# Output projection and queries in one block, a norm by one value per token, gate products written interleaved, and a later wait for the gathered tokens

## The reference, cut to what matters

```python
merged = sigmoid(z_ga) * (o_a @ w_o_attn) + sigmoid(z_gb) * (o_b @ w_o_lru)
x = x + gate1 * (merged @ w_out)                       # output projection
h2 = rms_norm(x, norm2_w) * (1 + scale2) + shift2      # norm over the 1024 channels of a token
q = (h2 @ w_q)                                         # 8 heads x 2 halves x 128: 16 query units
s = q . keys                                           # 128 scores per token, head and half
top_s, top_i = top_k(s, 16)                            # then 16 of the 16 x 16 pairs: expert, gate
act = gelu(h2 . u[expert]);  y = sum(gate * act * v[expert])
x = x + gate2 * y
```

## Time and profile before

| | us |
|---|---|
| three runs, median (lowest, highest) | 3951.05 (3950.67, 3953.24) |
| the profiled execution, its own time | 3958.0 |
| its span, first to last instruction | 3956.2 |
| PE busy | 3665.3 (93%) |
| DVE, ACT, POOL busy | 2632.0 (67%), 1363.8 (34%), 592.2 (15%) |
| mean granted PE clock, of full speed | 0.962 |

### The profile page before, as it was taken

The page is one execution under the profiler, slowest core; times in us unless marked ns, Lnnn a source line. Parts: engine busy times, 40 slices in busy tenths (PEclk is TensorE's granted clock), DMA queues, the critical chain, the costliest instruction groups (busy, mean ns, idle before and its releaser), DMA issues. The chain is left out here.

```text
span 3956.2 us, 60630 instructions
## 1 busy us (share of the span) xinstructions
PE 3665.3 (93%) x21828; PEld 3400.2 (86%) x21828; DVE 2632.0 (67%) x5338; ACT 1363.8 (34%) x1755; POOL 592.2 (15%) x516
## 2 busy tenths in 40 slices
PE   5999998897797897999999999999889999999999
PEld 2777776786586797999999999999889999999999
DVE  5134443588334686687777777777577877788887
ACT  3134343476212211233333342424233333333332
POOL 0000000000000000222222323231122222222221
PEclk8999999899798898999999999999999999999999
DMA  7311110110422112667776868595799999999997
GB/s 282 127 62 63 47 51 35 41 67 32 149 107 91 54 51 93 221 202 244 236 258 221 270 210 280 198 298 183 247 374 347 346 347 347 350 369 348 346 346 270
DMA packets 372800, 811.92 MB, mean 205 GB/s; under 512 B 30720, under 2 KB 207744, under 8 KB 369152
## 3 DMA queue, kind: packets, MB, share of 16 engines
q1 hardware_dynamic: 298880, 540.81, 38.9%
q0 software_dynamic: 73728, 268.47, 19.9%
HBM read 679.66 MB, written 129.50 MB: 205 GB/s over the span
## 5 line engine op out<-in xcount | busy, mean ns | idle before, releaser
L80 PE MATMUL s_ps_a<-back_dense_hi,s_u_hi 128*128 128x384 f32 x2048 | 708.9, 346 | 43.7 <-DVE s_u_lo L1648 26.8
L80 PE MATMUL c_ps_y<-c_wa_hi,c_v_hi 128*128 128x384 f32 x2048 | 686.6, 335 | 29.3 <-DVE c_wa_lo L1984 29.3
L82 PE MATMUL s_ps_a<-back_dense_hi,s_u_lo 128*128 128x384 f32 x2048 | 691.1, 337 | 0.0
L81 PE MATMUL s_ps_a<-back_dense_lo,s_u_hi 128*128 128x384 f32 x2048 | 690.8, 337 | 0.0
L81 PE MATMUL c_ps_y<-c_wa_lo,c_v_hi 128*128 128x384 f32 x2048 | 685.2, 335 | 0.0
L82 PE MATMUL c_ps_y<-c_wa_hi,c_v_lo 128*128 128x384 f32 x2048 | 685.1, 335 | 0.0
L1962 ACT ACTIVATE c_v_hi<-c_v_raw 128x1024 fp32r<-128x1024 f32 x256 | 271.7, 1061 | 658.2 <-PE c_ps_y L82 624.6
L1585 POOL DMA_INDIRECT s_row<-in_u_rows,back_expert x128 | 159.7, 1248 | 2045.1 <-DVE back_expert L1750 1603.7
L1982 DVE TENSOR_TENSOR c_v_lo<-c_v_raw,c_v_hi 128x1024 fp32r<-128x1024 f32 x256 | 313.7, 1225 | 195.3 <-ACT c_v_hi L1962 195.1
L80 PEld LDWEIGHTS s_ps_a<-back_dense_hi,s_u_hi 128*128 128x128 f32 x2048 | 390.2, 191 | 45.4 <-DVE s_u_lo L1648 27.0
L80 PEld LDWEIGHTS c_ps_y<-c_wa_hi,c_v_hi 128*128 128x128 f32 x2048 | 385.2, 188 | 30.4 <-issue 25.9
(11 more groups left out here) (329 smaller groups left out, 6704.2 us busy)
## 6 DMA issues: line engine op xcount, KB each, us to landing
c_v_raw<-in_v SPq DMA_DIRECT2D x256, 512.0 KB, 6.3
s_u_raw<-in_u SPq DMA_DIRECT2D x128, 512.0 KB, 4.9
act_scratch<-s_a SPq DMA_DIRECT2D x128, 384.0 KB, 3.9
gm_scratch<-s_gm SPq DMA_DIRECT2D x48, 1024.0 KB
c_a<-act_scratch SPq DMA_DIRECT2D x256, 192.0 KB, 3.5
c_g<-gm_scratch SPq DMA_DIRECT2D x256, 192.0 KB, 4.3
a_w<-in_w_ada SPq DMA_DIRECT2D x24, 1024.0 KB, 7.7
q_raw<-in_w_pq SPq DMA_DIRECT2D x17, 512.0 KB, 3.3
```

The costliest lines, as they stand in the source:

```text
L80: nc.tensor.matmul(out, w_hi, x_hi, start=first, stop=False)
L81: nc.tensor.matmul(out, w_hi, x_lo, start=False, stop=False)
L82: return nc.tensor.matmul(out, w_lo, x_hi, start=False, stop=last)
```

## The change

1. project and route become one block, project_and_route. Its buffers share space: q takes x's, the keys those of the square and the sum, all_best, all_place, tok and struck take chunks of x1.
2. The norm: eight products of total's token tiles by a column of ones give one sum per token; root and reciprocal are taken of 128 x 8 values; DVE spreads them (copy by broadcast), PE transposes 8 tiles into ps_rstd, and DVE multiplies the chunks by PSUM.
3. DVE interleaves the multiplication of chunk k + 2 with the low parts of chunk k, and PE runs the first query unit chunk by chunk (512 and 256 dense columns) behind them, then its gathered columns.
4. Query weights 8 and 9 (units 0 and 1) are loaded and split in the projection. Unit u's scores are made between the two banks of unit u + 1. The token tiles are transposed after unit 0 and in unit 1, both through score[:, 1].
5. top16 writes all_best itself; the seventeenth weight is no longer loaded (nor the tenth of w_out laid out again).
6. A gate product writes every fourth column of ps_g, so that ACT copies runs of four tokens.
7. combine: tok is loaded after chunk 0 and waited for before the first gathered row; PE waits for the identity only at the last chunk.

```diff
-def project(nc, io, keep):
-def route(nc, io, keep):
+def project_and_route(nc, io, keep):
+        ps_ms, ps_rstd = score[:, 0, 0:TT], score[:, 1]
+        keys = sums[:].rearrange("p a (u n) -> p (a u) n", n=NK)
+        q = x
+        all_best, all_place = (x1[:, n:n + 2].rearrange(...) for n in (0, 2))
+        @block.sync
+            def load(n):
+                if n >= LOADED + 2:
+                    sp.wait_ge(lo_done, n - LOADED - 1)
+                sp.dma_start(raw[:, n % 2], weight(n)...).then_inc(raw_in[n % 2], 16)
+            for n in range(KD):
+                sp.wait_ge(x1_done, n + 1)
+                sp.dma_start(io["x1_scr"][n], x1[:, n]).then_inc(stored, 16)
+            load(KD + LOADED)
+            load(KD + LOADED + 1)
+            sp.wait_ge(spread_done, 1)
+            sp.dma_start(keys, ...).then_inc(keys_in, 16)
+            for n in range(KD + LOADED + 2, WEIGHTS):
+                load(n)
+        @block.scalar
+            nc.scalar.activation(root[:], ps_ms, ACT.Sqrt, bias=eps[:], scale=1.0 / D).then_inc(root_done, 1)
...
+            for u in range(UNITS):
+                for c, (c0, c1) in enumerate(split_columns(T)):
+                    act.wait_ge(half_done, 2 * u + c + 1)
+                    if u >= 2:
+                        act.wait_ge(s_ready, u - 1)
+                    nc.scalar.activation(q[:, u % 2, c0:c1], acc[:, u % 2, c0:c1], ACT.Copy).then_inc(q_done, 1)
+                    if u == 1 and c == 0:
+                        token_rows(1)
+                if u + 2 < UNITS:
+                    high(KD + u + 2)
+                if u == 0:
+                    token_rows(0)
+        @block.vector
+            low(KD - 1 + LOADED)
+            dve.wait_ge(root_done, 1)
+            nc.vector.reciprocal(rstd[:], root[:]).then_inc(rstd_done, 1)
+            nc.vector.tensor_copy(spread..., rstd[:]....broadcast_to([P, TT, P])).then_inc(rstd_done, 1)
+            dve.wait_ge(stored, 16 * KD)
+            dve.wait_ge(spread_done, 1)
+            normalise(0)
+            normalise(1)
+            for k in range(KD):
+                if k + 2 < KD:
+                    normalise(k + 2)
+                for n, (hi, lo, tokens) in enumerate(halves(k)):
+                    dve.wait_ge(h2_hi_done, 2 * k + n + 1)
+                    nc.vector.tensor_tensor(lo, tokens, hi.bitcast(F32), ALU.subtract).then_inc(h2_lo_done, 1)
+            for u in range(UNITS):
+                if u + 2 < UNITS:
+                    low(KD + u + 2)
+                hold(dve, s_ready, u + 1, passed)
+                top16(... all_best[:, t, u, 8 * g:8 * g + 8] ...)
+                nc.vector.tensor_copy(all_place[:, :, u], place[:]).then_inc(kept, 1)
+        @block.tensor
+            for j in range(TT):
+                last = nc.tensor.matmul(ps_ms[:, j:j + 1], total[:, j * P:(j + 1) * P], ones[:], start=True, stop=True)
+            for j in range(TT):
+                last = nc.tensor.transpose(ps_rstd[:, j * P:(j + 1) * P], spread[:, j * P:(j + 1) * P], ident[:])
+            for k in range(KD):
+                pe.wait_ge(h2_lo_done, 2 * k + 1)
+                for c0, c1 in ((0, HALF), (HALF, TD)):
+                    last = query(0, k, c0, c1)
+            pe.wait_ge(h2_lo_done, 2 * KD)
+            for k in range(KD):
+                last = query(0, k, TD, T)
+            token_rows(0)
+            for u in range(1, UNITS):
+                pe.wait_ge(lo_done, KD + u - LOADED + 1)
+                if u >= 2:
+                    pe.wait_ge(q_done, 2 * (u - 1))
+                bank(u, 0).then_inc(half_done, 1)
+                if u == 2:
+                    pe.wait_ge(tok_done, GATHERED)
+                scores(u - 1)
+                if u == 1:
+                    pe.wait_ge(tok_done, 1)
+                    token_rows(1)
+                bank(u, 1).then_inc(half_done, 1)
+            scores(UNITS - 1)
+    nc.clear_and_free_semaphores(sems)
+    nc.all_engine_barrier()
...
-                        nc.scalar.activation(gm[:, :, g * GT:(g + 1) * GT].rearrange("p i t -> p t i"),
-                                             ps_g[:, g % 2].rearrange("p (t i) -> p t i", t=GT), ACT.Copy).then_inc(g_copied, 1)
+                        nc.scalar.activation(gm[:, :, g * GT:(g + 1) * GT],
+                                             ps_g[:, g % 2].rearrange("p (i t) -> p i t", t=GT), ACT.Copy).then_inc(g_copied, 1)
...
-                                last = nc.tensor.matmul(ps_g[:, g % 2, i * NK:(i + 1) * NK], one2[:, g % 2, i], one1[:, g % 2, i], start=True, stop=True)
+                                last = nc.tensor.matmul(ps_g[:, g % 2].rearrange("p (n t) -> p n t", t=GT)[:, :, i], one2[:, g % 2, i], one1[:, g % 2, i], start=True, stop=True)
...
-            for s in range(RING):
+            load(0, 0, 0)
+            sp.dma_start(tok[:], io["tok_scr"][1]).then_inc(tok_in, 16)
+            for s in range(1, RING):
                 load(0, s, s)
-            sp.dma_start(tok[:], io["tok_scr"][1]).then_inc(tok_in, 16)
...
-                    dve.wait_ge(tok_in, 16)
...
                         if h == 0:
+                            dve.wait_ge(tok_in, 16)
...
+                if last:
+                    pe.wait_ge(consts_in, 16)
...
-            pe.wait_ge(consts_in, 16)
...
-                project(nc, io, keep)
-            route(nc, io, keep)
+                project_and_route(nc, io, keep)
```

More of the change, by code:

```diff
@@ L1381, in _ @@
             act.wait_ge(ident_in, 16)
             nc.scalar.activation(ident_r[:], ident[:], ACT.Copy).then_inc(ident_done, 1)
[L1383 to L1397 removed]
+            act.wait_ge(summed, 1)
@@ new lines, in _ @@
+            nc.scalar.activation(root[:], ps_ms, ACT.Sqrt, bias=eps[:], scale=1.0 / D).then_inc(root_done, 1)
+            for k in range(KD + 1):
+                if k < KD:
+                    act.wait_ge(normed, k + 1)
+                    nc.scalar.activation(x1[:, k], x1[:, k], ACT.Identity, bias=keep.mod[:, 3 * KD + k:3 * KD + k + 1],
+                                         scale=keep.gain[:, 2, k:k + 1]).then_inc(modulated, 1)
+                if k >= 1:
+                    act.wait_ge(modulated, k)
+                    for hi, _, tokens in halves(k - 1):
+                        nc.scalar.activation(hi, tokens, ACT.Copy).then_inc(h2_hi_done, 1)
@@ L1419, in _ @@
         @block.tensor
         def _(pe):
-            pe.wait_ge(ident_done, 1)
-            for g in range(GATHERED):
+            for n in range(KD):
+                if n >= LOADED:
+                    pe.wait_ge(lo_done, n - LOADED + 1)
+                    pe.wait_ge(x1_done, n - 1)
                 for k in range(KD):
-                    out, tile = score[:, g, k * P:(k + 1) * P], (TD + g * P, TD + (g + 1) * P)
+                    for c0, c1 in split_columns(T):
+                        last = product3(nc, acc[:, n % 2, c0:c1], w_hi[:, n % 2, k], w_lo[:, n % 2, k], keep.mg_hi[:, k, c0:c1], keep.mg_lo[:, k, c0:c1],
+                                        k == 0, k == KD - 1)
+                last.then_inc(prod_done, 1)
@@ new lines, in query, with bank, token_rows @@
+            def query(u, k, c0, c1):
+                return product3(nc, acc[:, u % 2, c0:c1], w_hi[:, u % 2, k], w_lo[:, u % 2, k], *h2(k, c0, c1), k == 0, k == KD - 1)
+            def bank(u, n):
+                for c0, c1 in TOKEN_BANKS[n]:
+                    for k in range(KD):
+                        last = query(u, k, c0, c1)
+                return last
+            def token_rows(g):
+                for k in range(KD):
+                    out, tile = score[:, 1, k * P:(k + 1) * P], (TD + g * P, TD + (g + 1) * P)
@@ L2125, in layout @@
     out["w_out"] = again(chunks(a["w_out"][0], P), 2)
-    out["w_pq"] = again(chunks(a["peer_w_q"][0], P))
+    out["w_pq"] = chunks(a["peer_w_q"][0], P)
     out["keys"] = np.ascontiguousarray(a["peer_keys"][0].transpose(3, 0, 1, 2)).reshape(P, -1)
```

281 lines of the change are left out of this document (107 added, 174 removed).

## The result

The changed kernel takes 3910.21 us (median of 4 runs, 3908.56 to 3911.43), against 3952.14 us before (4 runs, 3950.67 to 3958.04). The ratio is 0.9891, interval 0.9874 to 0.9908: 42 us faster, where 26 were forecast, and 1.8 us under the lower end of the range.

What follows compares the result with a forecast made beforehand. TensorE, busy 93% of the span, was taken as the bound. Routing -17.4 us, gate products 0 and combine -8 made -25.4: 3932.6 for the profiled execution, 7 us less for the median, forecast as 3925; range 3912 to 3948.

Steps and rivals of the forecast that it cites:

- The norm: Start of the routing: first sum product to first multiplication takes 6.9 us instead of 10.7, 3.8 less.
- Chunks and first unit: Routing's start: last dense subtraction 20.2 us behind first multiplication, high clock from 1296.3, unit 1 at 1298.1 (1295.5 to 1300.5).
- Units: Routing's other query units: still 13.07 us each, moved scores counted as nothing; last query product 20.4 us earlier.
- The new tail: End of the routing: the moved scores make the last top-16 start later, 2.7 us given back.
- The boundary: End of the joint block: clearing semaphores and a barrier cost 0 to 0.8 us, taken as 0.3.
- Gate products: Gate stage: ScalarE's copy may fall from 1110 to 600 ns, worth nothing since ScalarE waits for TensorE; taken as 0.
- The strided write: Gate stage: TensorE writing PSUM at a stride of four elements costs 0, or about 20 us at 0.120 per pass.
- (b): Gate stage: the strided write runs at half rate and pays 0.120 us per pass, +20 us, 3945; chance 0.13.
- (c): Gate stage: the strided write doubles the pass, 0.101 to 0.2 us, +130 us, 4055; chance 0.15.
- Combine: Combine's start: first product 11.2 us earlier, 2.4 to 3 us lost at chunk 4; taken -8, bounds -3 and -11.
- Rival (a): Combine gains nothing, as TensorE's early start is lost to transfers; -17.4 us in all, 3933; chance 0.10.
- The sum: Whole kernel: routing -17.4 us and combine -8 make -25.4 us.

Runs made afterwards that it cites:

- Experiment 9: The changed kernel with a plain first query unit, started only when all chunks are split: 3917.83 us, ratio 0.9916 to the kernel before.
- experiment 8: The changed kernel with unit 14's scores issued ahead of unit 15's first half: 3905.56 us, ratio 0.9886 to the kernel before.
- experiments 1: The kernel before with the gate edit alone (interleaved write and copy in runs of four): 3933.87 us, ratio 0.9959.
- 2: The kernel before with only ScalarE's gate copy made contiguous, TensorE's write as before, gates left in another order: 3930.87 us, ratio 0.9950.
- 3: The kernel before with only TensorE's gate write at a stride of four, ScalarE reading strided and writing as before: 3950.39 us, ratio 1.0000.
- 4: The kernel before with only ScalarE's order changed, next weight copy ahead of the fourth gate copy and activation: 3914.04 us, ratio 0.9906.
- experiment 7: The changed kernel with combine's 2 MB load of x1 issued behind each pass's chunk loads: 3903.22 us, ratio 0.9879 to the kernel before.
- experiment 6: The changed kernel with gate and combine edits undone, leaving the joint block alone: 3931.50 us, ratio 0.9951 to the kernel before.
- experiment 5: The kernel before with the combine edit alone (c_tok issued fourth, later waits for it and the identity): 3948.60 us, ratio 0.9993.

## Why the prediction was wrong in size, point by point

- **The norm: right.** -3.8 forecast, -4.3 measured between the last projection product and the first multiplication (14.46 to 10.17 us). Scaling the first stage's rows held but for the sums (2.94 us, 3.5 forecast): root and reciprocal 0.27 and 0.20, spreading copy 0.69, transposes 1.94 us.
- **Chunks and first unit: right mechanism, the clock mis-sized.** The last dense subtraction ended 20.3 us behind the first multiplication (20.2 forecast), with VectorE pacing at 2.33 us for a chunk. But unit 1 began 26.2 us behind it, not 28.7. I had counted the clock's rise from the unbroken work near 1289.6. But at the low clock the six products of a chunk nearly fill VectorE's 2.33 us: from the first query product, 1272.32, TensorE works with no recorded wait for three chunks, and the clock rises in the third, 5.6 us after that product. The trace has 512-column products 0.43 us apart until 1277.91 and 0.24 apart from 1279.57 on. Only then, with the products shorter, does TensorE wait, before each of the next four chunks (0.45, 1.02, 1.02 and 0.80 us), and the granted clock stays at 0.99 over 1278 to 1287. The 24 gathered products took 2.9 us, the value for the high clock. Experiment 9 gives the interleaving 9.4 us.
- **Units: right.** 196.9 us from the start of unit 1 to the last scores (197.9 forecast); no product waits.
- **The new tail: right.** The last top-16 starts 5.14 us behind the last scores, VectorE ends 15.46 us behind them (15.4 forecast), and experiment 8 takes 2.75 us of it back. The boundary costs 0.6 us more, where 0.3 was taken.
- **Gate products: the step that failed** is "is worth nothing: ScalarE waits 324.3 us for TensorE there". The 324.3 us are a sum over the stage. At the end of each chunk ScalarE works without a pause, and there what comes off the copy comes off the start of `s_u_hi`, of `s_u_lo`, of `s_one` and of TensorE's late group (0.51 us off the copy, 0.42 us off the group's start). The row for the wait was in hand, 24.0 us in 42 pieces with VectorE as releaser; it was used only as a deduction from the strided write's price, and I did not ask what VectorE was waiting for. The runs showed 17.7 us gained where the term was 0: experiments 1 and 2 show the gain (16 and 19 us), 3 that the write has no part in it, and 4 that the order in ScalarE's queue is the cause, since with the weight copy ahead of the fourth, still long, copy only 0.8 of the 35.7 us are left. The remaining 4.5 us by which this stage differs between the two profiled executions are the clock between the bodies, and no step of the prediction.
- **The strided write: right at nothing.** Rivals (b) and (c) fall with experiment 3. The Trainium skill's page Advanced Engine Details and Errata, section Memory Cachelines, has it that non-contiguous PSUM access slows matmuls significantly; for these float32 passes of 128 columns the trace does not show it, 0.81 us for eight both ways. The same section says of SBUF that its lines have 16 bytes and that a different line at each access costs. With that the traces agree: ScalarE's copy of 512 values takes 1110 ns when each lands in another row of `s_gm` and 598 when four follow each other, that is 16 bytes.
- **Combine: right mechanism, mis-sized.** -11.3 us at the start (11.2 forecast), but the late chunk's price was not 2.4 to 3 us. From its first product to its end the stage takes 8.7 us longer than before. Against the same products of before, 0.8 us are lost at the second chunk, 3.7 at the fifth, and 2.5 because 16 products run at the low clock behind that wait (0.33 against 0.174 us each): 7.0 us from the edit. The other 1.6 us come between the two passes over the chunks. TensorE waits there in both kernels (3.70 us until 3419.12 before, 3.69 us until 3369.57 after), and the granted clock over the five microseconds behind it was 1.00 in the execution of before and 0.66 in that of after. It fell there too in experiment 6, where combine is the old one (its products behind the wait come 1.6 us later than those of before), so this is not the edit's. The prediction had the wait nearly right and did not price the clock. That x1 stands in front of the chunk's loads is shown by experiment 7, which leaves 0.9 of the 7.0. Rival (a), that combine gains nothing, was closer to the truth for this stage than my forecast of 8: alone, the edit gains 2.5 us, within noise of nothing (experiment 5).
- **The sum.** Stage by stage the errors were -3.7, -22.2 and +5.4, and -2.0 in code that did not change, 22.5 on the profiled executions. The medians moved 6 us less than the profiled executions: 4.5 us between the bodies and 2.0 before the projection came from the executions and not from the kernel. The range's lower end, 3912 or -39 us, is not made of the bounds that the prediction names: an earlier unit 1 (-2.6), a boundary that costs nothing (-0.3) and combine at -11 (-3) take -25.4 to -31. That the result lies only 1.8 us under the range is therefore luck and does not speak for the term of the gate stage, for which no bound and no rival allowed a gain.

## What to carry to other kernels

An engine's total idle time does not make its work free: look at the instructions that stand back to back in its queue just before the bounding engine waits, and follow each waiting engine to what it waits for itself. Price a stall from start to start against an undisturbed repeat, not from recorded idle time. Where a new order starts a stage sooner, look at which large transfer now stands in front of the next small one that is needed, and count the clock that can be lost behind a wait of some microseconds. Before a difference between two profiled executions is put down to an edit, compare the stretches that the edit does not touch.

## What the runs showed of the hardware that was not expected

- A recorded wait understates what is lost: 0.57 us recorded, 0.74 us between the starts of the groups, and 0.10 more at the group behind it (3.08 us instead of 2.98), 0.84 in all. Over the stage it is 24.0 us recorded against 35.7 lost.
- ScalarE's writes in runs of four float32 cost it no more than contiguous ones (598 against 600 ns, the change and experiment 2), and writes of one value to a row almost double (1110 ns). Reading PSUM with a stride of four adds nothing to that (1109 ns, experiment 3); whether it would cost beside a contiguous write no run shows.
- TensorE's granted clock rose 5.6 us after the first query product, in work without a recorded wait, and then stayed at 0.99 with waits of up to 1.02 us in each chunk of 2.33 us. Behind a single wait of some 3 us or more it fell in some cases and not in others, in the same code: 3.58 us at combine's fifth chunk and it fell to 0.53, 3.36 us there in experiment 9 and it stayed at 1.00; 3.00 us between two bodies and it fell, 3.14 us between the next two and it stayed. What decides is not shown here. With the old copy, the five stretches between the bodies differ by up to 10 us from one profiled execution to another.
